# Both heads of a pair exchanged by DMA and turned by VectorE in steps 34 to 51

## The chip, the cores and the metric

The kernel runs on one core of one Trainium2 chip. Its metric is the device time of one execution in microseconds (us), a median over runs. TensorE (PE in the profile) multiplies, VectorE (DVE), ScalarE (ACT) and GpSimd (POOL) do the elementwise work, and SyncE (SP) issues nearly all transfers; a transfer is issued in program order on its queue and carried out by 16 DMA engines.

## The reference

One layer of a transformer block on 1024 tokens of width 1024. A normed input is projected to two groups of attention heads. The second group, which the change touches, has 8 heads of width 64. Token chunks of 64 look at their own and the 8 chunks before:

```
def mixer_b(q, k, v, rel_table):
    qc = q.reshape(b, nc, CHUNK, B_HEADS, HEAD_DIM)
    kb = band_gather(k.reshape(b, nc, CHUNK, B_HEADS, HEAD_DIM), B_BAND)
    vb = band_gather(v.reshape(b, nc, CHUNK, B_HEADS, HEAD_DIM), B_BAND)
    logits = jnp.einsum('bcqhd,bckhd->bhcqk', qc, kb) * SCALE
    rel = jnp.clip(band_rel(B_BAND), -B_REL_CLIP, B_REL_CLIP) + B_REL_CLIP
    logits = logits + rel_table[rel].transpose(2, 0, 1)[:, None]
    logits = jnp.where(valid[:, None, :], logits, NEG)
    p = jax.nn.softmax(logits, axis=-1)
    out = jnp.einsum('bhcqk,bckhd->bcqhd', p, vb)
    return out.reshape(b, s, B_W)
```

Both groups' outputs go through an output projection, a norm, and then a squared-ReLU MLP of width 4096 with norms before and after. All is float32.

## The kernel before

The work is one long program, written out by hand for each engine, with semaphores between the engines. Tokens are cut into 8 tiles of 128 (T = 8, P = 128). Attention runs in 64 numbered steps. Steps 0 to 31 are the first group. From step 32 on, a step n is one pair of heads of the second group (n // 8) and one tile of queries (n % 8): its query tile sees `keys_of(n)` = 1, 2, 3, 4, 5, 5, 5, 5 blocks of 128 keys. A "full" step below is one with 5 blocks (640 keys). In steps 34 to 55, two consecutive steps with n % 8 below 4 are `paired`: the scores of both are multiplied in the even one.

Between the attention work of each step TensorE does filler: four triples of matmuls (12 of 128x512) of the projections for later head pairs (`fill`, in `three`, L2336 to L2338). Two steps' filler makes one half tile. From half 21 on (that is from step 32) all halves use one PSUM bank, bank 4. So the first filler matmul of an even step waits (`s_et`) until VectorE has taken the half before out of the bank: `take`, which is `tile_scaled`, L1684, an instruction that writes `tmp`.

What happens to one step n of 34 to 51 (`turned_b`), in order:

- TensorE: `scores(n)`, 12 matmuls (L2528) into PSUM, head 0 in banks 0 and 1, head 1 in banks 2 and 3.
- VectorE: `scores(n)` adds the bias and takes the minimum, once for each head (L1795). Head 0 is written back into PSUM, head 1 into `prob_b` in SBUF.
- ScalarE: `exp` for each head (L1244), which sums the rows, then VectorE's `reciprocal` (L1806).
- Normalising: head 0 by ScalarE (`normalize`, L1251), head 1 by VectorE (L1812).
- Transposing: head 0 is sent by SyncE in four transfers SBUF to SBUF (`exchange_step`, L819) from `prob_b` into a buffer of its own, `turn_in` (there are two, for even and odd steps). They put the 32x32 blocks into place, and VectorE turns them (`turn_probs`, L1827) into `probT_b`. The transfers wait for the normalised head (`s_pb`) and for the turning of step n - 2 that read the same `turn_in` (`s_tb`). Head 1 is transposed by TensorE, block by block (L2547), into PSUM, and copied to `probT_b` by ScalarE (L1228, four blocks) and VectorE (L1820, the fifth).
- TensorE: `weigh(n)` multiplies the turned probabilities by the values (L2565, the trace has 4 records for each key block, both heads together). In an odd step m it does `weigh(m-3)` and `weigh(m-2)`, one after the other, straight after `scores(m)`; its end is counted in `s_pv`.

`probT_b`, like `prob_b`, holds two steps: the even and the odd. Step 52 and later transpose both heads on TensorE.

VectorE's order in a step from 36 on is written in one loop: `take` (even steps only), `scores`, the two `normalize`, `turn_probs(n-1)`, the copy of step n - 1, the low half of the tile that was taken (`tile_lo`, L1697, even steps), and in every fourth step or so a split of weights (`wf_lo`, L1847, after ScalarE's `wf_hi`, L1282).

## Time and profile before

| | |
|---|---|
| median of 3 runs | 1027.0 us (1026.8 to 1027.26) |
| the profiled execution | 1027.07 us, its span 1025.3 us |
| TensorE busy | 1016.1 us, 99% of the span |
| VectorE, ScalarE, GpSimd busy | 767.8, 476.8, 220.0 us |
| share of TensorE in the chain that ended last | 95% |
| mean granted TensorE clock | 0.999 of full speed |
| steps 34 to 51 | about 180.5 to 271.9 us of the span |

The span is the time from the first to the last instruction on the core; 1.8 us of the execution lie around it. The timeline of an engine gives the start and duration of each instruction. On TensorE the durations overlap (a matmul starts before the one before has ended), so the time a group really takes is read from one group's start to the next group's start. The starts and durations of DMA issues on SP are those of the issuing queue; the landing of the data comes later and is listed apart.

### The profile page before, as it was taken

The numbers are of one execution on the slowest core, as the hardware profiler recorded it, in microseconds if no ns is written. First come the engines' busy times: TensorE is split into PE (matmuls) and PEld (weight loads), VectorE is DVE, ScalarE is ACT, GpSimd is POOL, SyncE is SP. The second block draws the span as 40 slices with busy tenths as digits, with TensorE's granted clock in tenths as the row PEclk, the third lists the DMA queues.
The fourth block names the chain that finished last, engine by engine and source line by source line (L and its number), as shares of the span: only waits on it lengthen the run. The fifth ranks groups of instructions, "written<-read, shape, count | busy, mean of one in ns | idle before, by whom it ended". The sixth has DMA issues, their size and how long they took to land.

```text
span 1025.3 us, 15760 instructions
## 1 busy us (share of the span) xinstructions
PE 1016.1 (99%) x5458; PEld 844.1 (82%) x5458; DVE 767.8 (75%) x1498; ACT 476.8 (47%) x990; POOL 220.0 (21%) x218
## 2 busy tenths in 40 slices
PE   9999999999999999999999999999999999999997
PEld 8899887777778888888888888888888888888886
DVE  4954678767787668888988777776454877778997
ACT  6622355656577568745311311311344444454562
POOL 5200000000000003168765765762100000000000
PEclk9999999999999999999999999999999999999999
DMA  9935442232171563046444344347777733464344
GB/s 200 229 97 134 109 127 70 84 112 82 50 227 42 164 186 124 21 165 226 175 156 149 148 163 152 141 160 234 233 247 240 226 93 100 136 197 142 93 139 171
DMA packets 145312, 152.32 MB, mean 149 GB/s; under 512 B 76984, under 2 KB 95680, under 8 KB 143184
## 3 DMA queue, kind: packets, MB, share of 16 engines
q1 hardware_dynamic: 144160, 151.08, 47.3%
q8 instruction: 44, 0.72, 0.3%
q14 instruction: 36, 0.29, 0.1%
q10 hardware_dynamic: 688, 0.20, 0.1%
q0 software_dynamic: 384, 0.04, 0.0%
HBM read 103.65 MB, written 47.49 MB: 147 GB/s over the span
## 4 chain that ended last, share of the span: by engine, by line
PE 95%; issue 2%; DVE 2%; ACT 1%; DMA 0%; DVEq 0%; SPq 0%; ACTq 0%
PE ps L2336 28%; PE ps L2338 28%; PE ps L2337 28%; PE ps L2565 2%; PE ps L2528 2%; PE ps L2547 2%; PE ps L2470 1%; PE ps L2505 1%; PE ps L2682 1%; PE ps L2684 1%; PE ps L2670 1%; DVE wc_lo L2012 1%; DMA xraw<-in_x 0%; ACT prob_b L1244 0%; PE ps L2700 0%
## 5 line engine op out<-in xcount | busy, mean ns | idle before, releaser
L2336 PE MATMUL ps<-b_hi,wc_hi 128*128 128x512 f32 x448 | 174.6, 390 | 0.2 <-DVE wc_lo L2012 0.2
L2337 PE MATMUL ps<-tm_lo,sm_hi 128*128 128x512 f32 (+1 forms) x450 | 174.6, 388 | 0.0
L2338 PE MATMUL ps<-tm_hi,sm_lo 128*128 128x512 f32 (+1 forms) x450 | 174.6, 388 | 0.0
L2336 PE MATMUL ps<-tm_hi,sm_hi 128*128 128x512 f32 (+1 forms) x450 | 174.6, 388 | 0.0
L2338 PE MATMUL ps<-b_hi,wc_lo 128*128 128x512 f32 x448 | 174.3, 389 | 0.0
L2337 PE MATMUL ps<-b_lo,wc_hi 128*128 128x512 f32 x448 | 174.3, 389 | 0.0
L1561 ACT ACTIVATE sm_hi<-sm_raw 128x512 fp32r<-128x512 f32 x112 | 70.7, 631 | 162.3 <-DMA sm_raw<-u_matrices 162.3
L2240 DVE TENSOR_TENSOR sm_lo<-sm_raw,sm_hi 128x512 fp32r<-128x512 f32 x112 | 78.1, 697 | 77.4 <-ACT sm_hi L1561 76.9
L2336 PEld LDWEIGHTS ps<-b_hi,wc_hi 128*128 128x128 f32 x448 | 84.1, 188 | 18.1 <-DVE wc_lo L2012 0.6
L2338 PEld LDWEIGHTS ps<-tm_hi,sm_lo 128*128 128x128 f32 x450 | 84.5, 188 | 17.5
L2336 PEld LDWEIGHTS ps<-tm_hi,sm_hi 128*128 128x128 f32 x450 | 84.5, 188 | 17.5
L2337 PEld LDWEIGHTS ps<-tm_lo,sm_hi 128*128 128x128 f32 x450 | 84.5, 188 | 17.3
L2337 PEld LDWEIGHTS ps<-b_lo,wc_hi 128*128 128x128 f32 x448 | 84.1, 188 | 17.5
L2338 PEld LDWEIGHTS ps<-b_hi,wc_lo 128*128 128x128 f32 x448 | 84.1, 188 | 17.4
L1473 ACT ACTIVATE p1s<-ps 128x512 f32<-128x512 f32 x16 | 9.6, 598 | 181.1 <-PE ps L2338 175.5
L2242 DVE TENSOR_TENSOR tm_lo<-w,tm_hi 128x512 fp32r<-128x512 f32 x112 | 76.7, 685 | 0.0
L2012 DVE TENSOR_TENSOR wc_lo<-up_raw,wc_hi 128x512 fp32r<-128x512 f32 x48 | 56.6, 1202 | 19.9 <-ACT wc_hi L1413 19.9
L2012 DVE TENSOR_TENSOR wc_lo<-wc_raw,wc_hi 128x512 fp32r<-128x512 f32 x64 | 69.0, 1080 | 2.5 <-POOL wc_raw L1107 2.5
L1570 ACT ACTIVATE tm_hi<-w 128x512 fp32r<-128x512 f32 x112 | 69.0, 616 | 0.0
L1099 POOL TENSOR_TENSOR wc_raw<-up_raw 128x512 f32<-128x512 f32 x16 | 22.4, 1401 | 216.1 <-DVE small L739 133.1
L2336 PE MATMUL ps<-x_hi,wf_hi 128*128 128x512 f32 x160 | 66.0, 412 | 0.5 <-DVE tmp L1684 0.5
L2338 PE MATMUL ps<-x_hi,wf_lo 128*128 128x512 f32 x160 | 62.6, 391 | 0.0
(266 smaller groups left out, 2053.5 us busy)
## 6 DMA issues: line engine op xcount, KB each, us to landing
u_matrices<-stage SPq DMA_DIRECT2D x112, 256.0 KB, 2.0
sm_raw<-u_matrices SPq DMA_DIRECT2D x112, 256.0 KB, 2.6
up_raw<-in_w_up SPq DMA_DIRECT2D x16, 1024.0 KB, 5.0
w<-in_w_down SPq DMA_DIRECT2D x64, 256.0 KB, 3.7
w_raw<-in_w_in SPq DMA_DIRECT2D x8, 512.0 KB, 3.7
xr<-in_x SPq DMA_DIRECT2D x8, 512.0 KB, 4.2
x_rows<-xr SPq DMA_DIRECT2D x8, 512.0 KB, 4.9
xf<-x_rows SPq DMA_DIRECT2D x8, 512.0 KB, 3.5
```

The source lines that it names most:

```text
L1099: nc.gpsimd.tensor_tensor(wc_raw[s][5][:], a21, a22, ALU.add).then_inc(s_wsum, 1)
L1561: nc.scalar.activation(sm_hi[r][:], sm_raw[r][:], ACT.Copy).then_inc(s_shi, 1)
L1570: nc.scalar.activation(tm_hi[r][:], down_weights[q][c][:], ACT.Copy).then_inc(s_thi, 1)
L2012: nc.vector.tensor_tensor(wc_lo[s][p][:], src, wc_hi[s][p][:].bitcast(F32), ALU.subtract).then_inc(s_wlo[s], 1)
L2240: nc.vector.tensor_tensor(sm_lo[r][:], sm_raw[r][:], sm_hi[r][:].bitcast(F32), ALU.subtract).then_inc(s_slo, 1)
L2242: nc.vector.tensor_tensor(tm_lo[r][:], down_weights[q][c][:], tm_hi[r][:].bitcast(F32), ALU.subtract).then_inc(s_tlo, 1)
L2336: pe.matmul(out, w_hi_, x_hi_, start=start, stop=False)
L2337: pe.matmul(out, w_hi_, x_lo_, start=False, stop=False)
L2338: return pe.matmul(out, w_lo_, x_hi_, start=False, stop=stop)
L2528: last = pe.matmul(score_of(n, hh)[:, c * width:(c + 1) * width], q[rows, tok], k[rows, keys], start=(i == 0), stop=(i == 2))
L2547: last = pe.transpose(ps[:, bank, i * P:(i + 1) * P], prob_of(n, hh)[:, c0 + k * P:c0 + (k + 1) * P], ident[:])
L2565: last = pe.matmul(out_, v_tok[:, 2 + 2 * (p - 4) + hh, t + 1 - nk + k], weighed_probs(n, hh, k), start=(k == 0), stop=(k == nk - 1))
```

## The change

In steps 34 to 51 head 1 goes the way of head 0. VectorE writes the biased scores of both heads back to PSUM, ScalarE takes the exponent of both into `prob_b` in the order of the four quarters, and ScalarE normalises both (so `s_pb` counts two for a step). One set of four transfers a step carries both heads: 1280 bytes instead of 640 for each partition and quarter in a full step. `turn_in` is gone; the transfers write into `probT_b` itself, where VectorE turns both heads in place by one instruction twice as wide. `chunks_of` gives no chunks for these steps, so TensorE has no transposes and ScalarE and VectorE no copies for them. There are 67 such transposes (one for each key block of head 1).

```diff
@@ chunks_of
     if turned_b(n):
-        return [(nk, nk, True)] if nk < B_KEYS else [(nk, 4, True), (nk + 4, 1, False)]
+        return []
@@
-        turn_in = [sb(f"turn_in{n}", at, [P, B_KEYS * P]) for n, at in enumerate((64, 204))]
@@
         def sent_probs(n):
 
-            return prob_of(n, 0)[:, 0:keys_of(n) * P]
+            return prob_b[:, 2 * (n % 2):2 * (n % 2) + 2].rearrange("p h n -> p (h n)")[:, 0:2 * keys_of(n) * P]
+
+        def sent_head(n, hh):
+            return sent_probs(n).rearrange("p (a h m) -> p h a m", a=4, h=2)[:, hh]
+
+        def turned_probs(n):
+            return probT_b[:, 2 * (n % 2):2 * (n % 2) + 2].rearrange("p h n -> p (h n)")[:, 0:2 * keys_of(n) * P]
@@ exchange_step(n), SyncE
-                m = keys_of(n) * 32
-                sp.wait_ge(s_pb, pb0 + turns_until(n + 1))
-                if n < TURNED_B[2]:
-                    sp.wait_ge(s_pv, A_STEPS)
-                else:
-                    sp.wait_ge(s_tb, tb0 + turns_until(n - 1))
+                m = keys_of(n) * 64
+                sp.wait_ge(s_pb, pb0 + 2 * turns_until(n + 1))
+                sp.wait_ge(s_pv, n - 1)
                 for a in range(4):
-                    sp.dma_start(turn_in[n % 2][32 * a:32 * a + 32, 0:4 * m].rearrange("j (c m) -> j c m", c=4),
+                    sp.dma_start(turned_probs(n)[32 * a:32 * a + 32, 0:4 * m].rearrange("j (c m) -> j c m", c=4),
                                  sent_probs(n)[:, a * m:a * m + m]).then_inc(s_pld[n % 2], 16)
@@ normalize(n), ScalarE
-                at = 2 * (n % 2)
-                act.wait_ge(s_ri, 2 * n + 1)
-                nc.scalar.activation(sent_probs(n), sent_probs(n), ACT.Copy, scale=rinv[0][:, at:at + 1]).then_inc(s_pb, 1)
+                for hh in range(2):
+                    at = 2 * (n % 2) + hh
+                    act.wait_ge(s_ri, 2 * n + hh + 1)
+                    nc.scalar.activation(sent_head(n, hh), sent_head(n, hh), ACT.Copy, scale=rinv[0][:, at:at + 1]
+                                         ).then_inc(s_pb, 1)
@@ turn_probs(n), VectorE
                 dve.wait_ge(*exchanged(n))
                 dve.wait_ge(s_pv, n - 1)
-                cols = slice(0, keys_of(n) * P)
-                nc.vector.transpose(prob_t(n, 0)[:, cols], turn_in[n % 2][:, cols]).then_inc(s_tb, 1)
+                nc.vector.transpose(turned_probs(n), turned_probs(n)).then_inc(s_tb, 1)
@@ VectorE's loop over the steps
-                if turned_b(n - 1):
+                if turned_b(n - 1) and n % 2 == 0:
                     turn_probs(n - 1)
@@
                 if n < LATE:
                     take_low(done)
                 splits(n)
+                if turned_b(n - 1) and n % 2:
+                    turn_probs(n - 1)
@@ scores(n), TensorE
                     if turned_b(n - 1):
-                        pe.wait_ge(s_exp, 2 * n - 1)
+                        pe.wait_ge(s_exp, 2 * n)
```

Three places in the order of instructions matter. The first is VectorE from the `take` of step 38 to the scores of step 39. Before (L1806 and L1812 normalise, L1827 turns step 37, L1820 copies a block, L1697 is the low half of the tile, the ISA rows are the bias and the minimum):

```order
L1827 STREAM_TRANSPOSE probT_b<-turn_in_94 128x640 [waits pv_done,value_halves_landed_then_even_probs_exchanged]
L1820 COPY probT_b<-ps 128x128 [waits pv_done,probs_transposed]
L1684 SCALAR_TENSOR_TENSOR tmp<-ps,rrow 128x512 [waits tile_halves_lo_ready,fill_halves_done]
L1794 MEMSET small 128x1 [waits scores_ready,probs_transposed]
L1795 ISA ps,small<-ps,bias_b 128x640
L1795 ISA small 128x1
L1794 MEMSET small 128x1
L1795 ISA prob_b,small<-ps,bias_b 128x640
L1795 ISA small 128x1
L1806 RECIPROCAL small<-small 128x1 [waits rstd_rows_then_exchanged_probs_ready,exp_ready]
L1806 RECIPROCAL small<-small 128x1 [waits probs_ready,exp_ready]
L1812 TENSOR_SCALAR prob_b<-prob_b,small 128x640 [waits rowsum_inverted]
```

The same place now, with the end of step 37 (L1819 turns step 36, L1677 is the `take`):

```order
L1799 RECIPROCAL small<-small 128x1 [waits rstd_rows_then_exchanged_probs_ready,exp_ready] x2
L1819 STREAM_TRANSPOSE probT_b<-probT_b 128x1280 [waits pv_done,value_halves_landed_then_even_probs_exchanged]
L1677 SCALAR_TENSOR_TENSOR tmp<-ps,rrow 128x512 [waits tile_halves_lo_ready,fill_halves_done]
L1787 MEMSET small 128x1 [waits scores_ready,probs_transposed]
L1788 ISA ps,small<-ps,bias_b 128x640
L1788 ISA small 128x1
L1787 MEMSET small 128x1
L1788 ISA ps,small<-ps,bias_b 128x640
L1788 ISA small 128x1
L1799 RECIPROCAL small<-small 128x1 [waits rstd_rows_then_exchanged_probs_ready,exp_ready] x2
```

The copy and the normalising of head 1 are gone, and the turning of the even step, twice as wide, stands directly ahead of the `take` of the next even step, in both versions.

The second is SyncE's queue at steps 36 to 38. Before:

```order
L819 DMA turn_in_94<-prob_b 32x4x160 [waits rstd_columns_ready_then_probs_turned,rstd_rows_then_exchanged_probs_ready]
L819 DMA turn_in_94<-prob_b 32x4x160 x3
L819 DMA turn_in_95<-prob_b 32x4x160 [waits rstd_columns_ready_then_probs_turned,rstd_rows_then_exchanged_probs_ready]
L819 DMA turn_in_95<-prob_b 32x4x160 x3
L790 DMA w_raw_88<-in_w_in 128x1024 [waits fill_halves_done]
L819 DMA turn_in_94<-prob_b 32x4x160 [waits rstd_columns_ready_then_probs_turned,rstd_rows_then_exchanged_probs_ready]
```

and now:

```order
L814 DMA probT_b<-prob_b 32x4x320 [waits pv_done,rstd_rows_then_exchanged_probs_ready]
L814 DMA probT_b<-prob_b 32x4x320 x3
L814 DMA probT_b<-prob_b 32x4x320 [waits pv_done,rstd_rows_then_exchanged_probs_ready]
L814 DMA probT_b<-prob_b 32x4x320 x3
L788 DMA w_raw_88<-in_w_in 128x1024 [waits fill_halves_done]
L814 DMA probT_b<-prob_b 32x4x320 [waits pv_done,rstd_rows_then_exchanged_probs_ready]
```

Nothing moved in the queue, but the wait for the turning two steps back has become a wait for the weighing two steps back (`pv_done`).

The third is TensorE in step 37 from the last of its scores on. Before (weighing of steps 34 and 35, then the transposes of step 36, then filler):

```order
L2565 MATMUL ps<-probT_b,v_tok 64x4x32
L2565 MATMUL ps<-probT_b,v_tok 64x128
L2547 MATMUL ps<-ident,prob_b 128x128 [waits probs_ready,probsT_by_act]
L2547 MATMUL ps<-ident,prob_b 128x128 x3
L2547 MATMUL ps<-ident,prob_b 128x128 [waits probs_ready,probsT_by_dve]
L2336 MATMUL ps<-x_hi,wf_hi_92 128x512
```

and now:

```order
L2559 MATMUL ps<-probT_b,v_tok 64x4x32 [waits rstd_columns_ready_then_probs_turned,probsT_by_dve,probsT_by_act]
L2559 MATMUL ps<-probT_b,v_tok 64x4x32 x5
L2559 MATMUL ps<-probT_b,v_tok 64x4x32 [waits rstd_columns_ready_then_probs_turned,probsT_by_dve,probsT_by_act]
L2559 MATMUL ps<-probT_b,v_tok 64x4x32 x7
L2330 MATMUL ps<-x_hi,wf_hi_92 128x512
```

The five transposes are gone, and the filler follows the weighing.

## Rows read from the trace of the kernel before

**Rows 1.** Windows: us, then PE, PEld, DVE, ACT, POOL busy, PEclk, DMA, GB/s.

```profile
200.00:232.00 32.00, 31.73 (x251) 25.04 (x251) 22.58 (x75) 19.13 (x45) 0.40 (x2) 1.00 0.36 106
243.00:270.00 27.00, 26.79 (x211) 21.38 (x212) 19.14 (x69) 16.72 (x41) 0.40 (x2) 1.00 0.32 95
```

**Rows 2.** Timeline of TensorE, steps 38, 39, 42 and 53 (start, us, operation, idle before).

```profile
200.10 0.42 PE L2528 MATMUL ps<-bk_hi,bq_hi 64*128 64x320 f32 x2
...
201.18 0.83 PE L2547 MATMUL ps<-ident,prob_b 128*128 128x128 f32 x5
202.28 0.51 PE L2336 MATMUL ps<-x_hi,wf_hi 128*128 128x512 f32 x1 [0.27 <-DVE tmp L1684]
...
205.20 0.42 PE L2528 MATMUL ps<-bk_hi,bq_hi 64*128 64x320 f32 x2
...
206.28 2.40 PE L2565 MATMUL ps<-probT_b,v_tok 128*64 128x128 f32 x40
208.61 0.76 PE L2547 MATMUL ps<-ident,prob_b 128*128 128x128 f32 x5
209.13 0.48 PE L2336 MATMUL ps<-x_hi,wf_hi 128*128 128x512 f32 x1
...
212.08 0.33 PE L2528 MATMUL ps<-bk_hi,bq_hi 64*128 64x128 f32 x2
...
221.97 0.44 PE L2528 MATMUL ps<-bk_hi,bq_hi 64*128 64x384 f32 x2
...
223.39 0.50 PE L2336 MATMUL ps<-x_hi,wf_hi 128*128 128x512 f32 x1
...
275.81 0.42 PE L2528 MATMUL ps<-bk_hi,bq_hi 64*128 64x320 f32 x2
```

**Rows 3.** Waits of steps 34 to 53 and of SyncE (total us, times, longest).

```profile
PE ps L2336 <- DVE tmp L1684: 0.5, 2, 0.3
SPq L819 <- ACT prob_b L1251: 37.7, 15, 4.6
```

**Rows 4.** Timeline of VectorE, end of step 35 and start of step 38.

```profile
189.60 0.58 DVE L1827 STREAM_TRANSPOSE probT_b<-turn_in 128x384 f32<-128x384 f32 x1 [0.64 <-DMA turn_in<-prob_b]
...
200.61 0.84 DVE L1827 STREAM_TRANSPOSE probT_b<-turn_in 128x640 f32<-128x640 f32 x1
201.37 0.25 DVE L1820 COPY probT_b<-ps 128x128 f32<-128x128 f32 x1
201.55 0.67 DVE L1684 SCALAR_TENSOR_TENSOR tmp<-ps,rrow 128x512 f32<-128x512 f32 x1
202.16 0.82 DVE L1795 CUSTOM_DVE_ANT_0 ps<-ps,bias_b 128x640 f32<-128x640 f32 x1
...
204.80 0.16 DVE L1806 RECIPROCAL small<-small 128x1 f32<-128x1 f32 x1 [0.65 <-ACT prob_b L1244]
```

**Rows 5.** Groups by line and shape (last: mean ns of one, idle before).

```profile
L1827 DVE STREAM_TRANSPOSE probT_b<-turn_in 128x640 f32<-128x640 f32 x8 | 6.7, 840 | 0.1
L1963 DVE STREAM_TRANSPOSE ps<-hs 128x1024 f32<-128x1024 f32 x4 | 5.0, 1260 | 1.3 <-DMA hs<-h_row_tiles 1.3
L2547 PE MATMUL ps<-ident,prob_b 128*128 128x128 f32 x81 | 13.0, 285 | 0.0
```

**Rows 6.** Timeline of ScalarE, step 37 and 38.

```profile
200.29 0.82 ACT L1251 ACTIVATE prob_b<-prob_b,small 128x640 f32<-128x640 f32 x1
...
204.67 0.82 ACT L1251 ACTIVATE prob_b<-prob_b,small 128x640 f32<-128x640 f32 x1
```

**Rows 7.** Timeline of SyncE: the four issues of step 37.

```profile
201.14 2.48 SPq L819 DMA_DIRECT2D turn_in<-prob_b  x4
```

**Rows 8.** DMA issues: KB each, median us from issue to landing.

```profile
bias_b<-bias_b_rep SPq DMA_DIRECT2D x8, 320.0 KB, 3.2
turn_in<-prob_b SPq DMA_DIRECT2D x32, 80.0 KB, 2.5
hs<-h_row_tiles SPq DMA_DIRECT2D x16, 128.0 KB, 2.8
turn_in<-prob_b SPq DMA_DIRECT2D x12, 48.0 KB, 2.0
```

More of the change, by code:

```diff
@@ L2611, in _ @@
                     weigh_a(n - 3)
[L2612 to L2617 removed]
+                if not paired(n - 1):
                     for c in range(min(2, len(chunks_of(n - 1)))):
```

44 lines of the change are left out of this document (13 added, 31 removed).

## The prediction

> **What bounds the kernel now.** I read the windows of the stretch that changes first. TensorE is busy 31.73 of 32.00 us and 26.79 of 27.00, at full clock, VectorE 22.58 of 32.00 (71%), ScalarE 19.13 [rows 1]. So TensorE sets the pace, and there is about 1% of idle time for the change to remove. Next, TensorE's timeline [rows 2]: an even full step (38) runs from 200.10 to 205.20: scores 1.08, transposes, a short wait for VectorE's `take`, then 12 filler matmuls from 202.28 to 205.20, 2.92. The odd step 39 runs to 212.08: scores 1.08, weighing of steps 36 and 37 2.33 (206.28 to 208.61), five transposes 0.52 (208.61 to 209.13), filler 2.95. Steps 38 and 39 together take 11.98 us. The one place where TensorE waits for another engine is the filler of an even step [rows 3]: 0.5 us in all, since `take` (start 201.55 to filler start 202.28, 0.73 us) stands behind the turning on VectorE [rows 2, 4]. That position is what the prediction hangs on.
>
> **What leaves TensorE.** 67 transposes. Five cost 0.52 us from start to start [rows 2], 0.104 each, so 67 x 0.104 = 7.0 us. The wait that goes with them in the even steps, a few tenths each, brings the most that can be saved to about 8 us.
>
> The Trainium skill (TensorE: Matmul & The Clock Gate, Part 4: PE-mode transpose) prices a transpose at about 275 ns in a kernel. The mean duration here is 285 ns [rows 5], which agrees, but the durations overlap. By the page's price 67 x 0.275 = 18.4 us would leave TensorE; by the starts it is 7.0, and I use the starts.
>
> **What changes on VectorE and ScalarE.** VectorE loses for a full step the normalising of head 1 and the copy (0.18 from start to start, 201.37 to 201.55) and turns 1280 columns instead of 640. 640 columns take 0.84 and 1024 take 1.26 [rows 5], 1.09 ns a column, so 1280 take about 1.54, or 1.46 to the next start (840 ns were 0.76: 200.61 to 201.37 [rows 4]). The two changes nearly cancel; its load is not the matter. ScalarE loses a copy and gains one more normalising, 0.72 to 0.82 [rows 6]; with 19.13 of 32.00 busy [rows 1] this costs nothing by load, but the set of transfers starts that much later after the exponent. TensorE's scores(n+1) now also wait for the exponent of head 1. In step 38 the minimum starts at 202.16 and the sum of head 1 is inverted at 204.80 [rows 4], so that exponent is over 2.5 us after the minimum began. Filler takes 2.92, so it hides this as long as the minimum starts with the filler, which it does (both follow `take`): cost nothing. Weighing reads strided operands for head 0 already; both heads' 40 matmuls take 2.33, so I put nothing there.
>
> **The wait that is added.** This is the main term. Before, SyncE issued the transfers of a step as soon as ScalarE had normalised: ScalarE's instruction of step 37 begins at 200.29 and lasts 0.82, the four issues begin at 201.14 [rows 6, 7], and all of SyncE's waits there name ScalarE [rows 3]. Now they write into `probT_b` and wait until step n-2 has been weighed. For an even n that happens in the odd step n+1, after its scores. The data then has to land, VectorE turns step n at the end of step n+1, and only behind that stands the `take` of step n+2, for which the even step's filler waits. That closes a ring from the end of one even turning to the next. For a full pair (38/39, 46/47):
>
> - `take` to filler 0.73 [rows 2, 4]; filler 2.92; scores 1.08; weigh(n-2) half of 2.33, 1.17 [rows 2];
> - end of weighing until SyncE issues: an estimate of 0.2, the tail by which a matmul's duration exceeds its distance to the next (half of it would be 0.1);
> - first to last of four issues: 2.48 for four, so 1.9 [rows 7];
> - landing of the last: 80 KB take 2.5, 128 KB 2.8, 320 KB 3.2 [rows 8]. A transfer is now 160 KB: between 2.5 (if bytes are free) and 3.2, I take 2.9, near the 128 KB row;
> - turning 1.46.
>
> Sum 0.73 + 2.92 + 1.08 + 1.17 + 0.2 + 1.9 + 2.9 + 1.46 = 12.36 us. TensorE alone would need for the pair 11.98 - 1.04 - 0.58 (the gap of 201.70 to 202.28) = 10.4 us. So the ring, not TensorE, is the bound, and it is a little longer than the 11.98 of before: each even step's filler will stand about 2 us behind its scores.
>
> For pairs 36/37 and 44/45 the step weighed first has three key blocks: 0.47 less, 11.89. Before, these pairs were shorter than 11.98, since the transposes of step 35 and 43 were already done in the paired steps; there the ring costs most.
>
> From the turning of step 38 to that of 42 (and 46 to 50), two pairs of short steps, TensorE's own work is the longer way for the first: 0.73 + 2.92 (filler 40) + 2.33 (weighing 38, 39) + 2.92 (filler 41) + 1.42 (scores 42 and 43, 221.97 to 223.39 [rows 2]) + 2.92 (filler 42) + 0.23 (weigh 40, four of 40 records of 2.33) + 0.2 + 1.9 + 2.35 (96 KB, a little above the 2.0 of 48 KB [rows 8]) + 0.9 (768 columns) = 18.82. I add 0.5 because in step 40 the split of weights (`wf_lo`) and step 39's turning push the turning of step 40 and with it the `take` of 42 behind the scores: 19.3.
>
> **The sum.** The first ring starts with step 34's turning, at 189.60 before [rows 4]. Its transfers now wait for a second normalising of 384 columns (0.5), land 0.35 later, and the turning takes 0.9: it ends at 191.35. Then 191.35 + 11.89 + 12.36 + 19.3 + 11.89 + 12.36 + 19.3 = 278.45 for the end of step 50's turning; `take` and filler of step 52, 0.73 + 2.92, bring the scores of step 53 to 282.1. Before they start at 275.81 [rows 2]. From there on nothing is changed, and the loads of the next stage are released by TensorE's own progress. So 6.3 us are lost: the 7 us of transposes are saved on an engine that then waits some 2 us in each of the even full steps and 52. On the profiled execution's own 1027.07 us this gives 1033.4; it stands at the median of the three runs (1027.0), so nothing is corrected.
>
> Bounds: landing at 2.5 (and 2.0 for the short steps) takes 0.4 off six passes, 2.3 us; half the tail 0.6; no 0.5 in the short steps 1.0. All together 1029.5. Landing at 3.2 adds 1.8; the load of 512 KB of weights, queued ahead of steps 38, 42 and 46, still running when they send, would add perhaps 0.5 each, 1.5: 1036.7.
>
> The Trainium skill (DMA: Bandwidth & Descriptors, Anatomy of one DMA) gives a transfer as 2.0 us plus bytes / 436 GB/s. The trace does not quite agree: 80 KB would be 2.2 and took 2.5 [rows 8]. By the page 160 KB take 2.4, the ring 11.85, and the sum 3.1 us less, 1030.3.
>
> **Rivals.** A: TensorE stays the bound and the saving arrives. It holds if the turned heads are there before the next `take` is due, that is, if the ring is under 10.4 us. It speaks for it that all of the exchange is hidden before (three waits of VectorE at most, such as the 0.64 at step 34's turning [rows 4]). Against it: 2 us would have to vanish from a sum of measured terms. It gives 1027.07 - 8 = 1019; half of it, if VectorE's place in the queue is less strict than I read, 1023. B: the ring binds but each term comes at its low end, and the two losses and gains cancel: 1026 to 1029. For it: six passes multiply each tenth. C: my forecast's ring, but VectorE's own queue closes it a second time: the odd step's transfers, sent only after the exponents and both normalisings, land behind the inverting of the sums in the next even step, so the odd turning and with it the minimum of the next odd step slip. In a step with `wf_lo` I find that landing about 1 us late and still covered by the ring; if it is not covered, four such steps add 1 us each: 1037.
>
> **How the numbers follow.** Forecast (the ring at 11.9 to 12.4): 0.65, C 0.13, B 0.12, A 0.10. The likeliest gives 1033.4. The range runs from 1028.5, which takes in the upper half of B, to 1037.5. A measurement of this kernel tells about 0.2%, 2 us, from no change: faster 0.12 (A and a bit of B), same 0.11, slower 0.77.
>
> **What would show it.** Right: TensorE's filler in steps 36, 38, 44, 46, 52 begins about 2 us after the scores end, released by the `take`, which follows directly on a turning of about 1.5 us that itself waited for the landing; SyncE's issues of even steps name TensorE's weighing as their releaser; steps 38/39 take 12.2 to 12.5; VectorE idles before the turning of the even steps. The L2547 records fall by 67. Wrong: if issues of even steps still name ScalarE, the added wait is not on the way, and A follows; if the landing of 160 KB is not between 2.5 and 3.2, the size is off by six times the difference; if TensorE waits at its scores rather than at the filler, the exponent of head 1 is the bound, which I put at nothing.

## The result, and the profile after

The changed kernel takes 1057.15 us, the median of four runs (1055.36 to 1058.12), against 1027.03 us for the kernel before on the same chip, also four runs: 1.0289 times as long, 95% interval 1.0274 to 1.0304. The prediction was 1033.4 us with a range of 1028.5 to 1037.5: slower, as it said, but by 30 us instead of 6, and far outside the range. The profiled execution took 1055.36 us with a span of 1053.5, a mean granted clock of 0.983; its rows are those shown here.

First the page: busy time, TensorE's granted clock in 40 slices, and the chain that ended last.

```profile
PE 1022.5 (97%) x5391; PEld 847.0 (80%) x5391; DVE 767.8 (73%) x1472; ACT 479.1 (45%) x990; POOL 220.5 (21%) x218
...
PEclk9999999888899999999999999999999999999999
...
PE 88%; DMA 3%; DVE 3%; issue 3%; SPq 1%; ACT 1%; POOL 0%; DVEq 0%; ACTq 0%; POOLq 0%
```

The chain now holds 3% of DMA, some 30 us, and the second row has four eights in the slices of the changed stretch. The prediction read the granted clock of the kernel before (1.00 [rows 1]) and never asked whether it would stay there. The windows (columns as in [rows 1]) show both losses side by side:

```profile
200.00:232.00 32.00, 23.85 (x164) 18.36 (x163) 16.78 (x48) 15.81 (x35) 0.40 (x2) 0.79 0.70 113
...
243.00:270.00 27.00, 20.82 (x144) 16.08 (x143) 16.71 (x40) 13.65 (x27) 0.00 (x0) 0.81 0.54 87
```

TensorE is busy 23.85 of 32 us where it was busy 31.73 [rows 1], and the clock granted to it is 0.79 where it was 1.00. Finer windows around two of the waits:

```profile
204.00:208.00 4.00, 1.56 (x4) 1.27 (x5) 3.69 (x8) 0.77 (x2) 0.00 (x0) 0.57 0.94 149
208.00:212.00 4.00, 4.00 (x14) 2.87 (x14) 2.32 (x4) 2.95 (x7) 0.00 (x0) 0.58 0.67 151
...
224.00:228.00 4.00, 4.00 (x10) 3.09 (x10) 2.59 (x9) 1.25 (x5) 0.40 (x2) 0.50 0.68 172
```

TensorE is fully busy from 208 to 212, at 0.58 of its clock: the chip grants it 1.2 GHz instead of 2.4 for most of the filler that follows a wait. The waits of steps 34 to 53 (total us, times, longest) answer [rows 3]:

```profile
DVE probT_b L1819 <- DMA probT_b<-prob_b: 26.5, 13, 5.3
...
PE ps L2330 <- DVE tmp L1677: 22.1, 7, 4.2
...
SPq L812 <- PE ps L2559: 59.4, 9, 9.2
```

The wait for `take` went from 0.5 to 22.1 us, in seven even steps (36, 38, 40, 44, 46, 48 and 52), and behind it VectorE waits for the landing of the pair that it must turn first. SyncE's releaser is now TensorE's weighing. That is the ring of the prediction. One pass of it on VectorE, from the `take` of step 38 to that of step 40 (the timeline, as [rows 4]), and TensorE's filler and weighing in it (as [rows 2]):

```profile
204.29 1.51 DVE L1819 STREAM_TRANSPOSE probT_b<-probT_b 128x1280 f32<-128x1280 f32 x1 [2.22 <-DMA probT_b<-prob_b]
205.73 0.65 DVE L1677 SCALAR_TENSOR_TENSOR tmp<-ps,rrow 128x512 f32<-128x512 f32 x1
...
221.05 1.51 DVE L1819 STREAM_TRANSPOSE probT_b<-probT_b 128x1280 f32<-128x1280 f32 x1 [5.28 <-DMA probT_b<-prob_b]
222.49 0.65 DVE L1677 SCALAR_TENSOR_TENSOR tmp<-ps,rrow 128x512 f32<-128x512 f32 x1
```

```profile
206.44 0.79 PE L2330 MATMUL ps<-x_hi,wf_hi 128*128 128x512 f32 x1 [3.27 <-DVE tmp L1677]
...
208.74 0.63 PE L2332 MATMUL ps<-x_hi,wf_lo 128*128 128x512 f32 x1
209.16 0.63 PE L2330 MATMUL ps<-x_hi,wf_hi 128*128 128x512 f32 x1
...
211.66 0.42 PE L2522 MATMUL ps<-bk_hi,bq_hi 64*128 64x320 f32 x2
...
212.73 2.40 PE L2559 MATMUL ps<-probT_b,v_tok 128*64 128x128 f32 x40
215.07 0.50 PE L2330 MATMUL ps<-x_hi,wf_hi 128*128 128x512 f32 x1
215.40 0.40 PE L2331 MATMUL ps<-x_lo,wf_hi 128*128 128x512 f32 x1
```

SyncE's issues, and the issue to landing of the transfers:

```profile
214.13 2.49 SPq L814 DMA_DIRECT2D probT_b<-prob_b  x4
```

```profile
probT_b<-prob_b SPq DMA_DIRECT2D x32, 160.0 KB, 4.1
...
probT_b<-prob_b SPq DMA_DIRECT2D x12, 96.0 KB, 2.7
```

Term by term, forecast and measured: `take` to filler 0.73 and 0.71 (205.73 to 206.44); filler 2.92 and **5.22** (206.44 to 211.66, 0.43 us from one matmul to the next instead of 0.23); scores 1.08 and 1.07; half the weighing and the tail 1.37 and 1.40 (212.73 to the issue at 214.13); first to last issue 1.9 and 1.89; landing of the last 2.9 and **5.03** (216.02 to 221.05); turning 1.46 and 1.44. The sum is 16.76 instead of 12.36. Five terms agree within 0.03 us. The 4.40 us are two terms: 2.30 in the filler, at half the clock, and 2.13 in the landing. The ring one pass earlier, from the `take` of step 36 (191.93) to that of step 38 (205.73), shows the landing without the clock: its filler took the usual 2.96, its last transfer landed after 4.75, and it lasted 13.80 instead of 11.89. Over the stretch, scores of step 53 begin at 304.02 instead of the forecast 282.1.

### The profile page after: what moved, and what is told of

Same layout as the page of the kernel before. It is cut to its first block, busy times and chain, and to the rows that moved or that the text cites. A ratio compares the mean times of both kernels' runs of the same rounds, so it can differ in the third digit from the quotient of the medians.

```text
span 1053.5 us, 15548 instructions
## 1 busy us (share of the span) xinstructions
PE 1022.5 (97%) x5391; PEld 847.0 (80%) x5391; DVE 767.8 (73%) x1472; ACT 479.1 (45%) x990; POOL 220.5 (21%) x218
## 4 chain that ended last, share of the span: by engine, by line
PE 88%; DMA 3%; DVE 3%; issue 3%; SPq 1%; ACT 1%; POOL 0%; DVEq 0%; ACTq 0%; POOLq 0%
PE ps L2330 26%; PE ps L2332 26%; PE ps L2331 26%; DMA probT_b<-prob_b 3%; PE ps L2559 2%; PE ps L2522 1%; SPq L814 1%; PE ps L2464 1%; PE ps L2541 1%; DVE wc_lo L2006 1%; PE ps L2499 1%; PE ps L2669 1%; PE ps L2671 1%; PE ps L2657 1%; DMA up_raw<-in_w_up 1%
## 5 line engine op out<-in xcount | busy, mean ns | idle before, releaser
L2330 PE MATMUL ps<-x_hi,wf_hi 128*128 128x512 f32 x160 | 71.3, 446 | 22.1 <-DVE tmp L1677 22.1
L2331 PE MATMUL ps<-x_lo,wf_hi 128*128 128x512 f32 x160 | 67.5, 422 | 0.0
```

The lines of the kernel that those rows point to most:

```text
L2330: pe.matmul(out, w_hi_, x_hi_, start=start, stop=False)
L2331: pe.matmul(out, w_hi_, x_lo_, start=False, stop=False)
```

## The experiments

What is to be tested: two causes, the half clock and the landing, add up to the whole miss. Rivals: the waits are what costs and the clock only accompanies them; the added wait, not the transfers, makes the ring; the order of the queue on VectorE makes it. Within the landing: bytes, packets, order, queue.

**The order of the transfers.**

```
-                for a in range(4):
+                for a in (0, 2, 1, 3):
```

> The changed kernel with one edit: the four transfers of a step are issued for the destination quarters 0, 2, 1, 3 of the partitions instead of 0, 1, 2, 3. In the changed kernel the four transfers of 160 KB take 4.3 us together (152 GB/s) and the last lands 4 to 5 us after its issue, where I had put 2.9. Theory P (ports: a transfer that writes only 32 partitions reaches few of the ways into SBUF, two in a row of the same half of the partitions share them, and the next queues behind): the last of four lands within 3.0 to 3.5 us of its issue, the ring of a full pair falls from 16.8 to about 13, the clock falls less often, and the time is 1036 to 1044. Rival S (the size of the packet: 1280 bytes from SBUF to SBUF are slow whatever they meet): landing stays 4 to 5 us and the time 1055 to 1058.

One run: 1057.46 us. The 160 KB transfers land in 4.1 us as before, and the `take` waits sum to 23.1 us. The order of the target partitions makes no difference.

**The turning behind the take.**

```
@@ VectorE's step n, after the minimum and the take
+                if n % 2 == 0 and turned_b(n - 2):
+                    turn_probs(n - 2)
@@ end of VectorE's step n
-                if turned_b(n - 1) and n % 2:
-                    turn_probs(n - 1)
```

> The changed kernel with one edit: VectorE turns an even step n not at the end of step n+1 but in step n+2, behind the take and the scores of that step. The transfers are untouched. Theory (the ring runs through VectorE's place in the queue: the filler waits for a take that stands behind the turning): the filler of the even steps no longer waits for the turning, TensorE is idle for under 0.5 us a pair, its clock stays at full, and the time is 1020 to 1030, what is left of the ring being exponent 1.75, scores 1.07, weighing 1.4, issues 1.9, landing 4.8, together 10.9 against TensorE's own 10.4. Rival (the place of the turning does not matter, the late landing holds up the exponents of step n+2, which reuse prob_b, just as much): the idle time only moves to the scores of the odd steps, and the time is above 1045.

One run: 1039.49 us, between the two expectations, which both missed. TensorE's waits in the stretch:

```profile
PE ps L2559 <- DVE probT_b L1819: 11.3, 7, 3.2
PE ps L2330 <- DVE tmp L1677: 1.1, 3, 0.6
```

22.1 us of waiting for `take` became 1.1, and 11.3 us of waiting for the turned pair at the weighing appeared. The longest waits of the weighing (3.2 us in step 39, 3.0 in step 47) stand in the middle of it, ahead of the odd step's half: VectorE idled 3.52 and 3.32 us there for the landing of that pair before it turned it. So the even turning's place ahead of `take` costs 18 us of the 30, the clock included, which is up from 0.983 to 0.993; behind it stands a second wait, for the odd pair, and the landing is in that one too.

**Half the bytes.** From step 38 on only head 0's 80 KB a transfer are sent; head 1's half of the turned buffer is left with old data. The output is therefore not the reference's.

```
-                    ...[32 * a:32 * a + 32, 0:4 * m].rearrange("j (c m) -> j c m", c=4), sent_probs(n)[:, a * m:a * m + m]
+                    sent = m // 2 if n >= 38 else m
+                    ...[32 * a:32 * a + 32, 0:4 * m].rearrange("j (c m) -> j c m", c=4)[:, :, 0:sent], sent_probs(n)[:, a * m:a * m + sent]
```

> The changed kernel with half the bytes in each transfer from step 38 on: head 0 is sent, head 1 is not (VectorE turns what lay there, so head 1's probabilities are those of step 36 or 37). Waits, number of transfers and all instructions are the same. Theory (my forecast with only the landing mis-sized): the last transfer lands 2.5 us after its issue, the rings of full pairs from step 38 on take 12 us, the time is 1030 to 1036. Rival (the clock falls as soon as TensorE idles some 2 us in each pair, so the ring itself is what costs, at whatever landing): landing 2.5 but filler of even steps still at half clock, rings 14 us, time 1042 to 1050.

One run: 1043.11 us. By its time this is the rival's range, so the trace has to tell. The landing (KB, median us) and the windows:

```profile
probT_b<-prob_b SPq DMA_DIRECT2D x24, 80.0 KB, 2.5
```

```profile
200.00:232.00 32.00, 26.19 (x203) 20.55 (x200) 19.08 (x51) 16.31 (x36) 0.40 (x2) 0.84 0.50 100
243.00:270.00 27.00, 22.64 (x180) 17.59 (x177) 19.56 (x52) 16.52 (x34) 0.00 (x0) 1.00 0.27 79
```

Up to step 40 the full transfers of 36 and 37 still delay it and the clock falls: the fillers of 36, 38 and 40 took 4.29, 5.07 and 4.54 us, some 5 us too much. Another 2.3 us of this one run were lost in its first 15 us, where its program is that of the changed kernel (the weighing ahead of step 35's filler began at 187.69 instead of 185.34). The rest, 1035.7, is in the range of the theory. From 42 on every filler runs at the full clock, which the rival excludes, and `take` to `take` is 11.49 us from step 44 to 46 (244.02 to 255.51) and 11.89 from 46 to 48 (255.51 to 267.40), where the recorded rings with 2.5 for the landing give 11.49 and 11.96. The ring was calculated rightly; what was put into it for the landing was not.

**TensorE kept busy.** 16 extra 128 x 512 matmuls ahead of the filler in every even step from 36 to 52:

```
+                if n % 2 == 0 and turned_b(n - 2) and n >= A_STEPS + 4:
+                    for _ in range(16):
+                        pe.matmul(ps[:, 5, 0:512], x_hi[:, 0, 0:P], x_hi[:, 0, 0:512], start=True, stop=True)
```

> The changed kernel with 16 matmuls of 128x512 added in each even step from 36 to 52 ahead of the filler, into a PSUM bank that nobody reads (3.6 us at full clock, where TensorE otherwise waits 2 to 4.2 us for the take). They leave the result as it is. Theory (part of the loss is the clock: it is granted at half after each wait, and the filler of the even steps takes 5.2 us instead of 2.9): the clock stays at full, each of some seven rings loses 2.3 us, and the time is 1039 to 1044, the rest of the loss being the landing. Rival (the clock falls for another reason, or the added work itself lengthens the rings): time within 3 us of 1057 or above.

One run: 1054.96 us, mean granted clock 0.999. The clock came back, but 16 matmuls are 3.75 us, more than TensorE waited in steps 36, 42, 44, 50 and 52, so they delayed these themselves. The time is in the rival's range for the reason that the rival names, the added work itself, and tells little about what the clock costs. The next one fits the number to the wait:

```
+AWAKE = {36: 8, 38: 12, 40: 14, 44: 7, 46: 13, 48: 14, 52: 7}
+                if n in AWAKE:
+                    for _ in range(AWAKE[n]):
+                        pe.matmul(ps[:, 5, 0:512], x_hi[:, 0, 0:P], x_hi[:, 0, 0:512], start=True, stop=True)
```

> The changed kernel with 128 x 512 matmuls without use put ahead of the filler of steps 36, 38, 40, 44, 46, 48 and 52: 8, 12, 14, 7, 13, 14 and 7 of them (0.234 us each at the full clock, so 1.9, 2.8, 3.3, 1.6, 3.0, 3.3 and 1.6 us), at most as long as TensorE waits there in the changed kernel; none in steps 42 and 50, where it waits for nothing. Earlier, 16 in every even step gave the full clock, but also made steps 36, 42, 44, 50 and 52 longer. If the half clock after the waits costs what the filler's durations add up to (12.9 us over 2.93 us a step), this gives 1057.2 - 12.9 = 1044 us with the fillers of 38, 40, 46 and 48 at 2.9 us; 1043 to 1047. If the half clock is only a sign of the waiting and costs nothing on the way, 1055 to 1058.

1043.7 us, four runs, ratio 1.0163 (1.0146 to 1.018).

```profile
200.00:232.00 32.00, 30.18 (x214) 23.00 (x212) 19.01 (x55) 16.45 (x38) 0.40 (x2) 1.00 0.74 127
```

```profile
202.91 3.03 PE L2612 MATMUL ps<-x_hi 128*128 128x512 f32 x12
206.19 0.50 PE L2331 MATMUL ps<-x_hi,wf_hi 128*128 128x512 f32 x1 [0.25 <-DVE tmp L1678]
206.53 0.40 PE L2332 MATMUL ps<-x_lo,wf_hi 128*128 128x512 f32 x1
```

The filler of step 38 begins a quarter of a microsecond earlier than in the changed kernel and each matmul then takes 0.23 us instead of 0.43. Work without any use, put into a wait, makes the kernel 13.5 us faster by the medians, and 11.8 between the two profiled executions. In the trace of the changed kernel the fillers of steps 38, 40, 44, 46, 48 and 52 took 5.22, 5.37, 4.53, 5.40, 5.42 and 4.54 us; that is 12.8 us over the usual 2.95 each. The clock is a cause, not a companion.

**The wait alone, in the kernel before.**

```
                 m = keys_of(n) * 32
                 sp.wait_ge(s_pb, pb0 + turns_until(n + 1))
+                sp.wait_ge(s_pv, n - 1)
```

> The kernel before with one part of the change alone: SyncE waits for the weighing of step n - 2 ahead of the four transfers of each step n from 36 on, as it must in the changed kernel where they write into the buffer that TensorE reads. The transfers stay 80 KB and go to turn_in. Forecast: 1027.0 to 1028.5 us, since the exchange of the kernel before has slack (its turning of an even step is ahead of the minimum by some microseconds and TensorE waits 0.5 us at most there). Rival: the wait itself makes the ring, and the time is 1033 us or more, as forecast for the whole change, with TensorE waiting at the filler for take_low.

1028.54 us, ten runs; ratio 1.0011 (1.0002 to 1.0021). What releases SyncE there is now the weighing, and still TensorE waits little (first SyncE's row, then TensorE's):

```profile
SPq L818 <- PE ps L2566: 30.0, 8, 5.0
```

```profile
PE ps L2337 <- DVE tmp L1685: 1.1, 2, 0.8
```

The added wait costs about 1 us by itself, as expected. It closes the ring, but with the transfers, the turning and the normalising of the kernel before in it the ring hardly binds. What the doubled turning costs without the doubled transfers was not run in a kernel that computes everything.

**Transfers by themselves.** Sets of transfers behind the last store of the kernel before, each begun when the one ahead had landed (the code for one set, shortened). A packet below is one piece that a DMA engine moves, as the trace records it; one of 1280 bytes is a row of the transfer.

```
+            for kind, m, split, first, second in PROBES:
+                eng.wait_ge(s_prb, done)
+                for a in (first, second)[mine]:
+                    ...
+                        d = probe_dst[32 * a:32 * a + 32, 0:4 * m].rearrange("j (c m) -> j c m", c=4)
+                        r = src[:, a * m:a * m + m]
+                    eng.dma_start(d, r).then_inc(s_prb, 16)
```

> The kernel before, unchanged, with sets of transfers from SBUF to SBUF put behind its last store, each set begun when the one ahead of it has landed; what they write is read by nothing. Set A is a full step's four transfers of 160 KB as the change sends them (128 partitions to 32, 1280 bytes a packet), B the four of 80 KB that the kernel before sends (640 bytes), C the bytes of A in eight transfers of 640 bytes a packet, E is A with the targets in the order 0, 2, 1, 3, F one transfer of A alone, M and N 1024 and 768 bytes a packet, D the bytes of A from 128 partitions to 128, G and H are A with two of the four issued by ScalarE (2 and 3, or 1 and 3), I is B in that way. In the trace of the changed kernel 512 packets of 1280 bytes took 4.3 us, 148 ns each, and the 640-byte packets of the kernel before 32 ns each. Theory 1 (a step's bytes into 32 partitions at a time are what is slow, whatever the queue and the packet): A 4.3 us, C the same or more, F 1.1 to 1.5, G and H 4 or more, D 2 or less. Theory 2 (the packet's length is what is slow, some length above 640 bytes): C 3.2 us or less against 4.3 for A, D as slow as A. Theory 3 (one queue holds them up): G and H 2.2 to 3 us, F as slow per byte as A. Theory 4 (it is the other work beside them in steps 36 to 51, the projection's weights and bias loads or the engines' traffic in SBUF): A here 3 us or less.

The times in the table below are from the first to the last packet of a set, and the packet's median, both from the trace's records of single packets. Windows over sets A, B, C, F and D (the last two columns are the DMA share and GB/s):

```profile
1030.00:1034.50 4.50, 0.00 (x0) 0.00 (x0) 0.00 (x0) 0.00 (x0) 0.00 (x0) 0.50 0.93 146
1036.70:1039.20 2.50, 0.00 (x0) 0.00 (x0) 0.00 (x0) 0.00 (x0) 0.00 (x0) 0.50 0.42 131
1041.00:1046.00 5.00, 0.00 (x0) 0.00 (x0) 0.00 (x0) 0.00 (x0) 0.00 (x0) 0.50 0.42 131
1054.30:1055.10 0.80, 0.00 (x0) 0.00 (x0) 0.00 (x0) 0.00 (x0) 0.00 (x0) 0.50 0.60 205
...
1067.10:1069.80 2.70, 0.00 (x0) 0.00 (x0) 0.00 (x0) 0.00 (x0) 0.00 (x0) 0.50 0.69 243
```

| set | us | packets, median ns |
|---|---|---|
| A: 4 x 160 KB to 32 partitions | 4.19 | 512 of 1280 B, 138 |
| B: 4 x 80 KB | 2.31 | 512 of 640 B, 32 |
| C: the bytes of A in 8 | 4.91 | 1024 of 640 B, 32 |
| E: A in the order 0, 2, 1, 3 | 4.19 | 512 of 1280 B, 138 |
| N: 4 x 96 KB | 2.37 | 512 of 768 B, 36 |
| M: 4 x 128 KB | 2.99 | 512 of 1024 B, 52 |
| F: one of A's | 0.64 | 128 of 1280 B, 56 |
| D: 4 x 160 KB to 128 partitions | 2.53 | 512 of 1280 B, 56 |
| G, H: A on two queues | 4.18, 4.15 | 138, 139 |
| I: B on two queues | 1.44 | 512 of 640 B, 32 |

A step's four transfers take the same 4.2 us with nothing else on the chip, so theory 4 is out. Two queues do not help, so theory 3 is out. D moves the same bytes in the same packets at the pace of the issues, 0.645 us each: a packet of 1280 bytes is not slow in itself, as theory 2 had it, and the narrow target is what matters. Theory 1 is right for A, C, G and H and wrong for F, which it put at 1.1 to 1.5 us, and for D, which it put at 2 or less. The issues of C come so slowly that its packets are never held up, so C doesn't tell whether short packets would help. I shows that the 80 KB transfers are paced by their issues too: from two queues the same four pass in 1.44 us, 228 GB/s. The query on one tile gives the landings, first those of set A, then that of F alone, min, median and max:

```profile
DMA to landing us min/median/max: 3.3/4.1/4.7
```

```profile
DMA to landing us min/median/max: 3.0/3.0/3.0
```

One transfer of 160 KB alone lands in 3.0 us. The prediction's 2.9 was the right price for one, and the wrong one for the last of four.

**Half of the transfers from ScalarE**, with the turning behind the take:

```
@@ exchange_step(n), SyncE
-                for a in range(4):
+                for a in (0, 1):
@@ exchange_step(n), ScalarE, at the end of its step
+                act.wait_ge(s_pb, pb0 + 2 * turns_until(n + 1))
+                act.wait_ge(s_pv, n - 1)
+                for a in (2, 3):
+                    act.dma_start(turned_probs(n)[32 * a:32 * a + 32, 0:4 * m]..., sent_probs(n)[:, a * m:a * m + m])
```

> The kernel that turns the even step's head pair behind the minimum and the take of the step after (1039.5 us earlier), with two of a step's four transfers issued by ScalarE at the end of its step instead of by SyncE. If the queue is what makes the last landing late (4.6 us instead of 2.9), the landing falls to 2.9 or less, the weighing of the odd steps stops waiting for the turning (11.3 us of waits there), and the time is 1022 to 1029 us. If it is the bytes into 32 partitions, the landing counted from the last issue stays over 4 us, but the last issue comes 1.2 us earlier, and the time is 1034 to 1039 us. If ScalarE's wait and its two issues of about 0.6 us a step delay the exponents, 1040 us or more.

1042.5 us, four runs, ratio 1.0151 (1.0136 to 1.0166): 3 us worse than with one queue. ScalarE's transfers land after 5.6 us, SyncE's after 4.6, and TensorE waits for exponents up to 1.0 us in four places (2.5 us in all), since ScalarE itself now waits at the issue (7.7 us in two places for the weighing). The last expectation came true.

**The transfers further apart.** F and A differ in whether one follows closely on another, which suggested that two at once are the trouble.

```
                 for a in range(4):
+                    for _ in range(5 if a and keys_of(n) == B_KEYS else 0):
+                        sp.wait_ge(s_pv, n - 1)
```

> The changed kernel with the four transfers of a step of five key blocks (steps 36 to 39 and 44 to 47 among them) issued further apart: ahead of the second, third and fourth SyncE has five waits that are already fulfilled. Bytes, packets, targets, queue and order are as in the changed kernel. In the probe a single transfer of 160 KB to 32 partitions took 0.64 us from its first packet to its last, but four of them issued 0.645 us apart took 4.19 us, the packets falling from 55 to 150 ns as soon as two were under way together; with 640 or 768 bytes a packet, or to 128 partitions, they did not. Theory (two such transfers at once get in each other's way, not the bytes): with at least 0.7 us between issues packets stay at 55 ns, the set ends 0.64 us after its last first packet, so from first issue to last landing it is 3 x 0.85 + 2.5 = 5.1 us instead of 6.9; 1.8 us less in each of some six rings that wait for it, about 11 us, and half a filler's slowness less where the wait gets short: 1036 to 1047 us. Rival (156 GB/s is what 32 partitions take, however it comes): the packets stay near 150 ns and the time is 1055 to 1059 us. If five fulfilled waits take no time, the issues stay 0.645 us apart and the run tells nothing.

1057.59 us, ratio 1.0288 (1.0271 to 1.0306), no gain. The first packets of the first two transfers came 0.74 us apart and the first was over when the second began; still the second slowed from 55 to 150 ns a packet halfway through, before the third had begun. The theory of a collision falls. With ten waits and the turning behind the take:

```
+                    for _ in range(10 if a and keys_of(n) == B_KEYS else 0):
+                        sp.wait_ge(s_pv, n - 1)
```

> The kernel that turns the even step's head pair behind the minimum and the take of the step after (1039.5 us earlier, with the weighing of the odd step waiting 11.3 us in all for the turned pair), with ten fulfilled waits between the four transfers of a step of five key blocks. If collisions of two transfers are what is slow, packets stay near 55 ns and the waits of the weighing shrink by 1 to 1.8 us each: 1028 to 1035 us. If the bytes are what is slow, 1039 to 1042 us. If ten waits take over 0.1 us each, the spacing eats the gain: 1038 to 1042 us with packets at 55 ns.

1040.2 us, ratio 1.0125 (1.011 to 1.014), against 1039.5 without spacing: the expectation of "the bytes". The issues of step 37's first two transfers are 0.90 us apart (201.77 and 202.67), so are their first packets (202.97 and 203.87), and the second transfer slows from about 204.3 on all the same.

**A second series of sets.** It was to tell a backlog from slow target groups.

> The kernel before with a second series of transfer sets behind its last store, each begun when the one ahead has landed; what they write is read by nothing. In the spaced kernel the second transfer of a set (to partitions 32 to 63) fell from 55 to 150 ns a packet in its second half although the first was over, so a collision of two is not what it takes. What fits both probes' rows so far is a backlog: short of about 110 KB ahead of what 133 GB/s would have carried since the set began, packets go at full speed, beyond it the set goes on at 133 GB/s. The sets: A as in the first probe (should be 4.2 us again). F1, F2, F3: one transfer of 160 KB alone, to partitions 32 to 63, 64 to 95, 96 to 127. S: four of them, all to partitions 0 to 31. W: four transfers of 160 KB to 64 partitions each. D2: eight of 160 KB to 128 partitions on two queues. C2: the bytes of A in eight transfers of 640 bytes a packet on two queues. K: four transfers from 32 partitions to the same 32, 5120 bytes a row. Theory (backlog of writes into few partitions at a time): F1 to F3 0.64 us each; A and S 4.2 us; C2 3.9 to 4.3 us, since 640-byte packets are held to 133 GB/s too when more are sent; D2 stays fast, 5.5 us or less for 1310 KB. Rival 1 (the second to fourth target groups are slow in themselves): F1, F2 or F3 0.9 us or more. Rival 2 (only packets over 768 bytes are slow): C2 2.9 us or less. W and K have no forecast by the theory other than that they lie between A and D: 2.6 to 4.2 us.

| set | us | GB/s |
|---|---|---|
| A again | 4.18 | 157 |
| F1, F2, F3: one alone, to 32 to 63, 64 to 95, 96 to 127 | 0.65, 0.67, 0.64 | 252, 246, 254 |
| S: four, all to partitions 0 to 31 | 4.18 | 157 |
| W: four to 64 partitions each | 3.94 | 166 |
| K: four from 32 partitions to the same 32, 5120 B a packet | 3.05 | 215 |
| D2: eight to 128 partitions, two queues | 3.82 | 343 |
| C2: 8 x 80 KB, two queues | 3.26 | 201 |

Rival 1 falls, since each target group alone is as fast as the first. A and S agree with the backlog: the first 1.3 or so transfers pass at full speed and the rest go at about 133 GB/s (the packets of 1031.2 to 1034.2 in the first series), whether they go to four groups of 32 partitions or all to the first. D2 shows that 128 partitions take 343 GB/s and more packets at once do no harm. C2, with 3.26 us, misses both expectations (3.9 to 4.3, and 2.9 or less): shorter packets are held up too, at 64 ns in the last quarter, but less. So rival 2 falls as well as the theory's single rate: what few partitions take depends on the length or the order of the packets, and W (two packets in a row to one partition instead of four) is hardly better than A. Which of the two it is was not separated, and why few partitions slow a set down stays open.

This is a place where the Trainium skill (SBUF — State Buffer, Door 1: The DMA port swizzle) speaks against the change: it says that partitions 0 to 31 reach 8 of 16 ports, that 0 to 63 reach no more, at most about 218 GB/s. The same page of the Trainium skill, in the section "Can I just issue two DMAs to hit both halves?", says that two transfers in parallel to different halves hardly add up (6% over a single one). The runs agree in kind: 64 partitions are 6% faster than 32 (W and S), G on two queues gains nothing, 128 partitions give twice the rate. In size they differ in both directions: one transfer alone runs at 254 GB/s, four together at 157. An estimate from the page, 655 KB at 218 GB/s, is 3.0 us for a set; it took 4.2.

**Both causes out.** Half the bytes from step 38 on (head 1's half is left with old data), and matmuls without use in the three even steps that the full transfers of 36 and 37 still delay:

```
+AWAKE = {36: 9, 38: 15, 40: 5}
+                    sent = m // 2 if n >= 38 else m
```

> The changed kernel with both causes taken out as far as can be: from step 38 on only head 0's bytes are sent (four transfers of 80 KB; its output is not the reference's, head 1's half of the turned buffer holds old data), and ahead of the filler of steps 36, 38 and 40 stand 9, 15 and 5 matmuls of 128 x 512 without use. Steps 36 and 37 still send all bytes. If the two causes add up, the half clock is gone (fillers 4.4, 5.2 and 4.6 us in the earlier run with half the bytes become 3.0 each) and the time is the earlier 1043.1 - 5.2 = 1038 us, 1036 to 1040; that is the recorded sum of 1033.4 plus about 2 us a ring for the landing of steps 36 and 37 and what the extra matmuls overhang. If there is a third cause of several us, it stays at 1041 us or more.

1036.87 us, median of four runs (1035.29 to 1041.98), ratio 1.0104 (1.0074 to 1.0135), as expected if there is no third cause. TensorE's waits and its windows:

```profile
PE ps L2332 <- DVE tmp L1679: 6.7, 5, 2.3
```

```profile
200.00:232.00 32.00, 30.68 (x224) 23.81 (x224) 20.89 (x65) 18.08 (x42) 0.40 (x2) 1.00 0.51 113
243.00:270.00 27.00, 23.46 (x190) 18.34 (x187) 18.84 (x51) 15.83 (x36) 0.40 (x2) 1.00 0.33 97
```

The clock is not out everywhere: behind a wait of 2.27 us the filler of step 52 still took 4.48, so 1.5 us of it are left. From the filler of step 42 to that of step 50, eight steps that stand for a whole turn of the pattern in every kernel:

| kernel | start of the fillers of steps 42 and 50 | us |
|---|---|---|
| before | 223.39, 264.36 | 40.97 |
| recorded ring (11.89 + 12.36 + 19.3) | | 43.55 |
| the same with the landings of the halved transfers (2.5, in the short step 2.1) | | 42.5 |
| changed | 235.26, 289.67 | 54.41 |
| kept busy, fitted | 230.74, 279.39 | 48.65 |
| half the bytes | 235.60, 279.45 | 43.85 |
| both causes out | 228.51, 270.96 | 42.45 |

Keeping TensorE busy takes 5.8 us off. Half the bytes, with which the clock stays up by itself here, take 4.8 more off. The last kernel, measured against the recorded ring with its own landings, fits within 0.1 us. The run with half the bytes is 1.35 us above it, and there TensorE's weighing of steps 47 and 49 waits for a turned pair:

```profile
PE ps L2560 <- DVE probT_b L1820: 1.6, 2, 1.2
```

In the last kernel these two waits are absent; what sets them off was not looked for. No further cause of several us shows in these eight steps.

## Why the prediction was wrong

**Right: the ring.** Slower came true by the mechanism that was named, not by luck: TensorE waits at the filler of the even steps, released by `take` behind the turning, and SyncE's issues are released by the weighing. The list of the waiting fillers (36, 38, 44, 46, 52) leaves out 40 and 48, where two of the longest waits are (4.23 and 4.04 us), although the full rings of the recorded sum end exactly there. The five terms of matmul, issue and turning hold within 0.03 us; 1280 columns took 1.51 us for the estimated 1.54.

**Right: what was put at nothing.** VectorE's load is the same (767.8 us before and after) and ScalarE's 2.3 us more (479.1), and the exponent of head 1 holds up the scores by 0.7 us in all. Rival A (TensorE stays the bound) is refuted by the 22.1 us of waits, B by the ring of 16.76. Rival C, VectorE closing a second ring, is not there in the changed kernel, but becomes real as soon as the first is opened: in the run with the turning behind the take an odd turning slips (that of step 37 to 208.61), and with it the weighing that reads it and the minimum behind it (210.68). Waits of this kind are most of the 11.3 us.

**Wrong: "landing of the last", 2.9 between bounds of 2.5 and 3.2.** It measured 5.03 (5.01 from issue to landing; 4.75, 4.99 and 4.82 in steps 36, 44 and 46). The step that failed is the choice of rows. All of [rows 8] are medians over transfers, and a bound was drawn through their sizes, as if only the size of one mattered. What was needed is a set's rate: the kernel before sends 4 x 80 KB in 2.48 us [rows 7], about 130 GB/s; the changed one asks 32 partitions at a time for 655 KB in the same 2.5 us, 260 GB/s, and they take 157. The text named "bytes are free" as a bound and checked the other end against 320 KB from DRAM to 128 partitions, a target four times as wide. In the four full rings this is 1.85, 2.11, 2.09 and 1.92 us. The short steps' 96 KB, put at 2.35, landed after 2.83, 2.82 and 2.84 in steps 34, 42 and 50, half a microsecond more in each. Together this is 9.4 us. The page's formula that the prediction quotes from the Trainium skill (DMA: Bandwidth & Descriptors, Anatomy of one DMA) would have missed by more: it stands there for a transfer issued through GpSimd, these are issued by SyncE, and it gives 2.4 for what took 3.0 alone and 4.7 to 5.0 as the last of four. Its effect on the sum was also reckoned too high, 3.1 us instead of 2.3, since two of the six passes are short steps.

**Wrong: the clock at 1.00.** The filler was taken over from a timeline in which TensorE hardly waits (0.27 us in step 38 [rows 2]). The same prediction said that TensorE would wait some 2 us in each of five steps, and did not ask what the 12 matmuls behind a wait cost. They took 5.2 to 5.4 us behind waits of 3.3 to 4.2 (steps 38, 40, 46, 48), 4.5 behind 1.95 and 1.96 (44 and 52) and 2.96 behind 2.39 (36); in the run with half the bytes the filler of step 36, behind a wait of 2.41, took 4.29 us, so the length of the wait alone doesn't tell. By the trace it is 12.8 us, by the fitted run 13.5, the largest single piece of the miss. It also multiplies the first error: in the run with half the bytes the waits stayed at 1.3 us or less after step 42, and the clock at 1.00. One wrong term of 2 us brought a second of the same size with it, in the same ring. It need not have been right even with the landing as forecast: in the kernel with both causes out a wait of 2.27 us, about the size that the prediction had named, was followed by a filler of 4.48.

The sum, from the trace of one execution: 1033.4 forecast, plus 9.4 from the landings, plus 12.8 from the fillers, is 1055.6; that execution took 1055.36, the median is 1057.15. The runs agree: with the clock at full the kernel is 10.3 us above the forecast (1043.7), and 3.5 with the bytes halved from step 38 on as well (1036.87). The range was too narrow although its bounds were carried through six passes: the landing's upper bound came from rows with another target width and load, and a cause that the text didn't weigh has no bound at all.

None of the variants beats the kernel before. The best that computes everything, with the turning behind the take, is 1039.5 us.

## What to carry to other kernels

When a change lengthens transfers inside a ring, price the set that is in flight together against the partitions that it writes, not one transfer by its size, and ask at which rate the issues would offer the bytes. When a forecast makes TensorE wait, recompute the matmuls behind the wait at both of its clocks: here waits of 3.3 to 4.2 us cost 2.3 to 2.5 us more in the 12 matmuls that followed. A ring that has been calculated from rows can be tested by taking each doubted term out alone; the rest then has to fit to a few tenths.

## What the runs showed of the hardware

- SBUF to SBUF into 32 partitions: one transfer of 160 KB passes in 0.64 us (254 GB/s), four issued 0.645 us apart take 4.14 to 4.19 us (about 157 GB/s), in either order, and the same when all four go to partitions 0 to 31; from two queues 4.15 and 4.18. To 128 partitions the same four take 2.53 us, eight of them on two queues run at 343 GB/s.
- The packets themselves go from 55 to some 150 ns after about one and a third transfers, and with a spacing of 0.74 or 0.90 us still before the second is over, although the first is done by then.
- Waits that are already fulfilled are cheap on SyncE: five of them widened the distance of two transfers' first packets from 0.645 to 0.74 us, ten to 0.90.
- Useless matmuls in a wait made the kernel 13.5 us faster (1057.15 to 1043.7), with the mean granted clock up from 0.983 to 0.998. The same 12 matmuls take 2.95 us at 1.00 of the clock and up to 5.42 behind a wait.
